# Two edits to a two-layer diffusion backbone kernel: the first modulation's chunks taken in pairs among the first columns, and the last tile's second half summed before the first half is scaled

## What is computed

```python
def adaln(cvec, w_ada, b_ada):
    return jnp.split(jax.nn.silu(cvec) @ w_ada + b_ada, 6, axis=-1)

sh1, sc1, g1, sh2, sc2, g2 = adaln(c, w_ada[l], b_ada[l])
hm = rmsnorm(x, norm_pre_mix[l]) * (1 + sc1) + sh1
... = hm @ w_in[l]
...
return x + g2 * rmsnorm(swiglu(hf, w_ffn_gate, w_ffn_up, w_ffn_down), norm_post_ffn)
```

## Time and profile before

| | |
|---|---|
| median of 3 runs | 2115.37 us (2115.2 to 2117.08) |
| the profiled execution's own time | 2116.27 us |
| its span | 2114.5 us |
| TensorE busy | 2092.1 us, 99% of the span |
| VectorE busy | 1558.5 us, 74% |
| ScalarE busy | 937.1 us, 44% |
| DMA | 246.05 MB, 116 GB/s on average; 317 GB/s in the first of 40 slices |

### The profile page before, as it was taken

How to read it: one execution, slowest core, us unless ns; L and a number is a source line. 1 busy time by engine, 2 the same in 40 slices (tenths; PEclk the granted TensorE clock), 3 DMA queues, 4 the chain that set the end, 5 groups by cost and what they waited for, 6 DMA issues and landing times.

```text
span 2114.5 us, 33751 instructions
## 1 busy us (share of the span) xinstructions
PE 2092.1 (99%) x13850; PEld 1993.0 (94%) x13850; DVE 1558.5 (74%) x2493; ACT 937.1 (44%) x1490; POOL 101.6 (5%) x195
## 2 busy tenths in 40 slices
PE   8999999999999999999999999999999999999998
PEld 6999999899989999999899999999999899999997
DVE  6688767777757887887877776755854688787786
ACT  6555432476335432333485554235743553233333
POOL 0000001110000000000000000011100000000000
PEclk9999999999999999999999999999999999999999
DMA  8333355324333222222433333532233312222223
GB/s 317 110 120 122 103 174 176 138 93 148 102 131 119 80 80 80 80 80 88 162 132 120 115 109 131 169 127 79 86 120 130 130 61 80 80 80 82 97 82 139
DMA packets 63241, 246.05 MB, mean 116 GB/s; under 512 B 7792, under 2 KB 8080, under 8 KB 60400
## 3 DMA queue, kind: packets, MB, share of 16 engines
q1 hardware_dynamic: 42480, 158.55, 21.6%
q0 software_dynamic: 20608, 85.35, 11.6%
HBM read 230.20 MB, written 13.66 MB: 115 GB/s over the span
## 4 chain that ended last, share of the span: by engine, by line
PE 93%; DVE 3%; ACT 2%; DMA 1%; issue 0%; DVEq 0%; POOL 0%; POOLq 0%
PE unit L502 11%; PE unit L503 11%; PE unit L504 11%; PE unit L514 10%; PE unit L517 10%; PE unit L515 10%; PE sc L502 4%; PE sc L503 4%; PE sc L504 4%; PE tp L502 4%; PE tp L503 4%; PE tp L504 4%; PE tp L862 1%; PE sc L838 1%; PE unit L889 1%; PE unit L888 1%
## 5 line engine op out<-in xcount | busy, mean ns | idle before, releaser
L1773 DVE TENSOR_TENSOR wl<-raw,wh 128x1024 fp32r<-128x1024 f32 x200 | 242.2, 1221 | 119.3 <-ACT wh L1224 117.3
L514 PE MATMUL unit<-hmh,wh 128*128 128x320 f32 x1056 | 318.5, 309 | 1.8 <-DVE vl L1783 1.5
L515 PE MATMUL unit<-hml,wh 128*128 128x320 f32 x1056 | 318.1, 309 | 0.0
L1224 ACT ACTIVATE wh<-raw 128x1024 fp32r<-128x1024 f32 x200 | 206.0, 1050 | 99.6 <-DMA raw<-w_main 99.5
L517 PE MATMUL unit<-hmh,wl 128*128 128x320 f32 x1056 | 240.6, 309 | 0.0
L1872 DVE CUSTOM_DVE_ANT_0 junk<-ada,csb,par 128x1024 f32<-128x1024 f32 x160 | 205.6, 1285 | 29.3 <-DMA ada<-w_ada 9.7
L514 PEld LDWEIGHTS unit<-hmh,wh 128*128 128x128 f32 x1056 | 198.3, 188 | 2.4 <-issue 2.4
L515 PEld LDWEIGHTS unit<-hml,wh 128*128 128x128 f32 x1056 | 198.3, 188 | 0.0
L502 PE MATMUL unit<-wh,hmh 128*128 128x256 f32 (+1 forms) x544 | 178.8, 329 | 0.3 <-DVE wl L1773 0.3
L503 PE MATMUL unit<-wl,hmh 128*128 128x256 f32 (+1 forms) x544 | 177.7, 327 | 0.0
L504 PE MATMUL unit<-wh,hml 128*128 128x256 f32 (+1 forms) x544 | 177.7, 327 | 0.0
(11 more groups left out here) (472 smaller groups left out, 5431.6 us busy)
## 6 DMA issues: line engine op xcount, KB each, us to landing
raw<-w_main SPq DMA_DIRECT2D x276, 512.0 KB, 3.8
ada<-w_ada POOLq DMA_DIRECT2D x80, 512.0 KB, 4.5
first<-w_first SPq DMA_DIRECT2D x8, 1024.0 KB, 19.2
x<-x_keep POOLq DMA_DIRECT2D x3, 2560.0 KB, 11.1
bias<-biases POOLq DMA_DIRECT2D x32, 192.0 KB, 2.7
x_keep<-x POOLq DMA_DIRECT2D x10, 512.0 KB, 2.9
bias<-biases POOLq DMA_DIRECT2D x16, 256.0 KB, 4.1
gains<-g_rows POOLq DMA_DIRECT2D x4, 1024.0 KB, 6.1
```

Source lines behind the costliest of these rows:

```text
L514: pe.matmul(u[:, h, 0:n], a[0], xs[h][0], start=f, stop=False)
L515: pe.matmul(u[:, h, 0:n], a[0], xs[h][1], start=False, stop=False)
L1224: act.activation(wh[slot[i]][:, :], raw[slot[i]][:, :], ACT.Copy).then_inc(w_hi[slot[i]], 1)
L1773: dve.tensor_tensor(wl[slot[i]][:, :], raw[slot[i]][:, :], f32(wh[slot[i]][:, :]), ALU.subtract)\
```

## The change

TensorE's loop goes over chunks 3 and 4, then 5 and 6, then 7 alone. For a pair it issues step 0 of the older chunk, both chunks' sums, step 1 of the older chunk, step 0 of the next chunk, both turns, and step 1 of the next chunk. For chunk 7 the order is as before. At the end, the sum of the last tile's features 512 to 1023 moves ahead of the multiplication of features 0 to 511 by the gains.

```diff
@@ -676,11 +676,18 @@
             pe.wait_ge(first_mod, 2)
-            for c in range(COLUMN_LAG, KD):
+            for c in range(COLUMN_LAG, KD, 2):
+                both = range(c, min(c + 2, KD))
                 first_step(0, c - COLUMN_LAG)
-                first_sums(c)
+                for a in both:
+                    first_sums(a)
                 first_step(1, c - COLUMN_LAG)
-                turn_rows(c)
+                if len(both) == 2:
+                    first_step(0, c + 1 - COLUMN_LAG)
+                for a in both:
+                    turn_rows(a)
+                if len(both) == 2:
+                    first_step(1, c + 1 - COLUMN_LAG)
@@ -2506,9 +2513,9 @@
                     dve.tensor_tensor(mix[:, t, halves_of_tile[0]], U.tile()[:, 0, :], mix[:, t, halves_of_tile[0]], ALU.add).then_inc(bank_free, 1)
-                    gained(t, halves_of_tile[0])
                     u = U.get()
                     U.release(dve.tensor_tensor(mix[:, t, halves_of_tile[1]], u[:, 1, :], mix[:, t, halves_of_tile[1]], ALU.add))
+                    gained(t, halves_of_tile[0])
                     gained(t, halves_of_tile[1])
```

## The result

The changed kernel takes 2117.94 us in the median of 22 runs, the kernel before 2115.55 us in 22 runs beside it: a ratio of 1.0013, with a 95% interval of 1.0007 to 1.0019. It is slower by 2.4 us, which is within the 0.2% that the prediction calls the same. The profiled execution took 2119.35 us with a span of 2117.6 us, so it is one of the longer ones. The runs of the changed kernel fall into two groups: 13 lie between 2117.3 and 2118.1 (median 2117.77), 9 between 2118.98 and 2120.81 (median 2119.48), and none between. The kernel before has no run above 2117.1 in its 22.

The account below looks back on a forecast made before the run. TensorE, busy 99% of the span, was taken as the bound, its start set by a VectorE and ScalarE chain. 2.15 + 0.24 = 2.4 us later on the median 2115.37 gave 2117.8 us, range 2115.2 to 2119.5.

Parts of the forecast that it names:

- The share of the start: Paired chunks at the program's head: low part of chunk 7 starts 2.15 us later, at 44.80, handed on in full.
- 0.72 us from a turn to its modulation: Head of the program: time from TensorE's turn to VectorE's modulation, used to place the modulations of chunks 3 and 5.
- The share of the end: Last tile: second gains overfill VectorE's 0.33 us wait for ScalarE's root, so the reciprocal starts 0.24 us later.
- The wait for chunk 4: TensorE reaches chunk 4's sums at about 24.96 and stands until 27.03 for their load: 2.07 us.
- the 26.98 of one profile: Landing time of chunk 4's load, issued at 6.38 and landing 20.6 us later, read before the change.
- The chain over VectorE: Head: chunk 5's modulation waits for its turn until 37.02, then VectorE's 2.84 us a chunk puts chunk 7's at 42.70.
- TensorE's own saving of 0.6 us: Both pairs save TensorE some 0.3 us each in changes between kinds of work, but the chain does not run through it.
- The first rival: Chunk 4's load is there in time; chunk 7's modulation only 0.1 to 0.7 us later, total 2115.7 to 2116.3; chance 0.15.
- The times that the prediction named for the changed trace: Head: modulation of chunk 3 at about 30.6, of chunk 7 at about 42.7, low part of chunk 7 near 44.8.
- the granted clock of 1.00: Sign expected in the changed trace: TensorE's granted clock stays full despite the new pause.
- the third rival: TensorE's clock falls in the pause before chunk 4's sums, costing about 1.9 us more: 4.3 in all, 2119.7; chance 0.07.
- What takes a delay on: After the head: no DMA wait in TensorE's list, so the 2.15 us later start is counted in full to the end.

Follow-up runs that it names:

- the pause filled: The whole change plus 20 transposes of the identity on TensorE between the sums of chunks 3 and 4: 2117.79 us, ratio 1.001 to the kernel before.
- the pairs alone: The changed kernel with the last tile's order as it was before: 2119.26 us, ratio 1.0015 to the kernel before.
- without the wait: Paired order, last tile as before, but sums of chunks 4 and 6 read the loads of chunks 3 and 5: 2115.61 us, ratio 1.0001 to the kernel before.
- the sums first: Kernel before, but from chunk 5 on each round runs sums, step 0, turn, step 1, with no pair: 2114.39 us against 2115.39, ratio 0.9994.
- the last tile alone: Kernel before with only the last tile's sum of half 1 moved ahead of half 0's gains: 2115.63 us, ratio 1.0001.

## Why the prediction was right, and where not

**The total.** Forecast 2117.8, measured 2117.94, and the lower group 2117.77. The share of the start, 2.15 us, was measured as 2.4 in the kernel with the pause filled, where the sums of chunk 4 began 3.34 us behind those of chunk 3 and not 2.97 as in the working; less that 0.37, it is 2.0. Of the 0.15 that is left the working has most in one term: it takes 0.72 us from a turn to its modulation, and in the profiles of the pairs it is 0.53 to 0.57 (31.94 to 32.51 after). The share of the end was 0.24 forecast and 0.25 measured. That the median came within 0.2 us of the forecast is in part luck: 13 of 22 runs happened to lie in the lower group, and in the pairs alone, where 3 of 11 did, the median was 2119.26.

**The wait for chunk 4.** It stands at the forecast place with the forecast releaser. It was 2.37 and 1.88 us in the two profiles, 2.07 in the working: the landing differs by half a microsecond from one execution to the next, so the 26.98 of one profile was good to about that.

**The chain over VectorE.** That TensorE's own saving of 0.6 us would not count holds: without the wait the pairs cost and gain nothing (18.59 and 18.59 us). That the modulation of chunk 5 waits for its turn and VectorE's 2.84 us a chunk decide from there holds in every profile of the pairs. The first rival, "chunk 4 is there in time", gave chunk 7's modulation 0.1 to 0.7 us later than before; in the kernel without the wait it stands 16.50 us behind chunk 3's sums, before 16.49. The times that the prediction named for the changed trace (30.6, 42.7 and 44.8) were passed in the profile after (32.51, 44.66 and 46.76), by 1.9 to 2.0 us, and the granted clock of 1.00 was not met: 0.54 us are the later landing (27.57, not 27.03), 1.50 the two steps at half the clock, which is the third rival, and the shorter way from turn to modulation takes 0.15 off.

**The clock: the step that failed.** I weighed the third rival down to 0.07, because at the end of the program the clock stayed full for 4 us after the last matmul, and the new pause was to be 2.1 us. It was taken as if a pause shorter than that were safe. It was not: a pause of 1.88 or 2.37 us was followed by half the clock in both profiles, once when TensorE began again and once a microsecond later, while it worked. By the times about half of the runs with the pause are in the upper group. One row at the end of one execution could not show this, and that row was one of the longest of its kind: over the eight profiles the granted clock falls 2.5 to 4.5 us after the last matmul's end, 4.4 before and 2.8 after. What the prediction had of the Trainium skill ("TensorE: Matmul & The Clock Gate", "Part 1: The HAM clock gate"), that idleness brings the throttled state back, is what both profiles show (0.50 after the pause). The same section says of the change to full speed that its point varies from run to run, with where the first matmul falls; the two profiles, with the fall at 27.1 and at 28.6, show such a spread for the fall. The price was nearly right: 1.9 us forecast, 1.71 between the medians of the groups, 2.2 in the pairs alone. Its source is less sure than the prediction says: over the slow first transposes (9.34 to 14.5) the granted clock of the rows reads 1.00, so that they ran at half the clock is inferred from their pace alone. With both sums the forecast should have been two values, 2117.8 and 2119.5, with a chance of about a half each by what is known now, and the median could have come out near either.

**What takes a delay on.** I wrote that no wait on a DMA stands in TensorE's list and that a later start is therefore handed on in full. The conclusion holds for the medians to some 0.4 us (with the pause filled, 2.4 at the start and 0.25 at the end cost 2.2; with the sums first, 1.0 sooner gained 1.0), the reason not for a single execution. Behind one of TensorE's two waits for the values' low parts stands a load that VectorE waits for. Before, and in the kernel with the last tile alone:

```profile
89.65 1.28 DVE L1872 CUSTOM_DVE_ANT_0 junk<-ada,csb,par 128x1024 f32<-128x1024 f32 x1 [5.91 <-DMA ada<-w_ada]
```

```profile
88.66 1.29 DVE L1872 CUSTOM_DVE_ANT_0 junk<-ada,csb,par 128x1024 f32<-128x1024 f32 x1 [3.95 <-DMA ada<-w_ada]
```

In the two profiles where VectorE waited about 6 us for it (before, and the pairs alone with 6.06), TensorE's second wait of 0.4 to 0.5 us is there; in the six with 3.82 to 5.32 it isn't. The chain that ended last agrees: it runs through that load in those two profiles and in none of the six; no run was made to test it. From the last low part's start to the last matmul's start took 2065.4 us before, 2064.1 after, and 2064.1 to 2065.1 in the six other kernels, whether early or late. So the profile of before was a long one, and the spans of two single profiles differ by 3.1 us where the start alone differs by 4.1.

## What to carry to other kernels

Before an engine's work on a loaded tile is moved ahead, subtract the landing of that load from the time at which the engine will get there; a load used 0.5 us after it lands has no more than that to give. Grouping like work saves its switches only for the engine that sets the pace; where a chain runs over two other engines in a fixed order, the order that hands them their next input soonest wins, and here it was worth 1.0 us with no instruction added or removed. An instruction moved into the gap in which an engine waits is free only up to the length of that gap: 0.33 us of wait did not hold 0.69 us of work. A pause of TensorE has two prices, its own length and the clock that may fall behind it; here a pause of 2 us was free of the second in about half of the runs only, and filling it with transposes of the identity took that second price away.

## What was not expected of the hardware

After a stop of TensorE of about 2 us, half the clock was granted for 3.4 us in both profiles of it, and the times say the same of about half of the runs; in one of the profiles the clock fell only after a microsecond of renewed work; at the end of the program the clock fell after 2.5 to 4.5 us without work, over eight profiles. One load of 1 MB landed at 27.0 in one execution and about half a microsecond later in another (issued at 6.4, landing 20.6 and 21.1 us behind it), with 402 to 425 GB/s on the DMA engines around it.
